# Second attention: one head of each pair normalised by GpSimd, the last piece of the transposed weights copied by VectorE, a new order on VectorE; the convolution in five PSUM banks

## The reference, cut to what matters

```python
for each of 16 heads, for the "selected" and the "window" branch:
    logit = q @ k.T + bias                       # 512 x 512, causal
    p     = softmax(logit)
    o    += gate[head, branch] * (p @ v)
# third branch: 31 compressed keys per query, softmax, gate, @ v_cmp
o = concat(heads) @ w_o
```

## Time and profile before

| | us |
|---|---|
| median of 3 runs | 1904.03 (1902.29 to 1905.01) |
| the profiled execution | 1903.93 |
| its span | 1902.1 |
| TensorE busy | 1876.1 |
| VectorE busy | 985.3 |
| ScalarE busy | 759.2 |
| GpSimd busy | 755.7 |

### The profile page before, as it was taken

How to read it: one execution, slowest core, us unless ns; L and a number is a source line. 1 busy time by engine, 2 the same in 40 slices (tenths; PEclk the granted TensorE clock), 3 DMA queues, 4 the chain that set the end, 5 groups by cost and what they waited for, 6 DMA issues and landing times.

```text
span 1902.1 us, 25390 instructions
## 1 busy us (share of the span) xinstructions
PE 1876.1 (99%) x9404; PEld 1536.4 (81%) x9404; DVE 985.3 (52%) x1647; ACT 759.2 (40%) x1306; POOL 755.7 (40%) x321
## 2 busy tenths in 40 slices
PE   9999999999999999999999999999999999999998
PEld 8887788888888888888888888898766688888886
DVE  7766379354345643335433434754798443443444
ACT  7777454222233532233222222433599632222221
POOL 2321434544444345444544443455300144454452
PEclk9999999999999999999999999999999999999999
DMA  5111313323232134963333232234011123223231
GB/s 205 56 56 34 96 53 112 111 90 101 96 99 91 65 104 93 197 165 100 100 104 99 95 99 89 78 121 147 21 34 57 45 78 111 89 90 107 90 98 57
DMA packets 52526, 177.55 MB, mean 93 GB/s; under 512 B 5559, under 2 KB 5943, under 8 KB 52440
## 3 DMA queue, kind: packets, MB, share of 16 engines
q1 hardware_dynamic: 48240, 166.22, 26.7%
q10 hardware_dynamic: 4200, 10.15, 3.6%
HBM read 166.88 MB, written 9.47 MB: 93 GB/s over the span
## 4 chain that ended last, share of the span: by engine, by line
PE 83%; issue 7%; DVE 5%; ACT 2%; POOL 2%; DMA 0%; DVEq 0%; POOLq 0%
PE ps L445 25%; PE ps L447 25%; PE ps L446 25%; PE ps L963 2%; POOL WL L405 2%; PE ps L904 1%; PE ps L986 1%; DVE arena L2349 1%; DVE arena L2324 1%; ACT arena L1183 1%; PE ps L580 1%; DVE arena L1729 1%; ACT arena L1139 1%; PE ps L877 0%; PE ps L977 0%
## 5 line engine op out<-in xcount | busy, mean ns | idle before, releaser
L405 POOL TENSOR_TENSOR WL<-raw,WH 128x1024 fp32r<-128x1024 f32 x291 | 726.7, 2512 | 1071.6 <-ACT WH L1048 1071.5
L1048 ACT ACTIVATE WH<-raw 128x1024 fp32r<-128x1024 f32 x293 | 302.2, 1054 | 496.2 <-PE ps L447 452.3
L445 PE MATMUL ps<-XH,WH 128*128 128x512 f32 (+1 forms) x1280 | 493.3, 385 | 1.9 <-POOL WL L405 0.8
L447 PE MATMUL ps<-XH,WL 128*128 128x512 f32 (+1 forms) x1280 | 491.1, 384 | 0.0
L446 PE MATMUL ps<-XL,WH 128*128 128x512 f32 (+1 forms) x1280 | 491.1, 384 | 0.0
L445 PE MATMUL ps<-HH,WH 128*128 128x512 f32 x1080 | 423.3, 392 | 0.8 <-DVE HL L2061 0.8
L447 PE MATMUL ps<-HH,WL 128*128 128x512 f32 x1080 | 420.5, 389 | 0.0
L446 PE MATMUL ps<-HL,WH 128*128 128x512 f32 x1080 | 420.3, 389 | 0.0
L445 PEld LDWEIGHTS ps<-XH,WH 128*128 128x128 f32 x1280 | 240.8, 188 | 52.1 <-POOL WL L405 2.9
L447 PEld LDWEIGHTS ps<-XH,WL 128*128 128x128 f32 x1280 | 240.7, 188 | 47.9
L446 PEld LDWEIGHTS ps<-XL,WH 128*128 128x128 f32 x1280 | 240.9, 188 | 46.7
(11 more groups left out here) (268 smaller groups left out, 1719.3 us busy)
## 6 DMA issues: line engine op xcount, KB each, us to landing
raw<-in_weights SPq DMA_DIRECT2D x299, 512.0 KB, 3.5
tab<-arena ACTq DMA_DIRECT2D x1, 5120.0 KB, 76.5
arena<-tab SPq DMA_DIRECT2D x16, 256.0 KB, 2.9
ftab<-arena ACTq DMA_DIRECT2D x1, 2080.0 KB, 23.4
h<-in_xT SPq DMA_DIRECT2D x8, 256.0 KB, 6.4
out_T<-h SPq DMA_DIRECT2D x8, 256.0 KB, 2.2
raw<-in_weights SPq DMA_DIRECT2D x4, 256.0 KB, 4.8
arena<-ftab ACTq DMA_DIRECT2D x4, 256.0 KB
```

What stands on the lines that cost most here:

```text
L405: nc.gpsimd.tensor_tensor(WL[:, s, :], raw[:, s, :], WH[:, s, :].bitcast(f32), SUB)\
L445: nc.tensor.matmul(out, wh, xh, start=start, stop=False)
L447: return nc.tensor.matmul(out, wl, xh, start=False, stop=stop)
L1048: nc.scalar.activation(WH[:, s, :], raw[:, s, :], ACT.Copy).then_inc(*m["whi"].tick())
```

## The change

- **Second attention, GpSimd:** the four multiplications that normalise the second head (r = 1) of each job go from VectorE to GpSimd, which waits for the reciprocals and counts in a new semaphore, n2_pool. The reciprocals of both heads stay on VectorE.
- **Second attention, third copy:** the 256-wide copy of each head goes from ScalarE to VectorE (pair_copy_last), with its own semaphore pt_last.
- **Second attention, order on VectorE:** turn n is now: reciprocal and normalisation of n-1's first head, reciprocal of the second, all three logit steps of n, the two third copies of n-1, then c_weights or the split. In the first job the last logit step moves in between the second and the third c_sub.
- **First attention:** the normalisation of n-1's first head moves in front of logits step 0 of n.
- **Convolution:** five banks (4, 5, 6, 0, 1) instead of three; a wait for the last users of banks 0 and 1 is put ahead of the second query projection.
- **Embedding gate:** two identity products instead of eight.
- **First feed-forward:** the two weight units are rounded before the root.

```diff
         KN, KRR = (5, 6, 0, 1), 7
+        CBANK = (4, 5, 6, 0, 1)
@@ gpsimd, after the keys' six subtractions @@
+            for n in range(NP):
+                pool.wait_ge(sems["i2_done"], 2 * n + 2)
+                for qs in range(TT):
+                    a = PAIRS[n].p(n, 1)[:, POFF[qs]:POFF[qs] + P * (qs + 1)]
+                    c = INV + 8 * (n % 2) + 4 + qs
+                    gate = 3 * PAIRS[n].heads[1] + 1 + PAIRS[n].br
+                    nc.gpsimd.tensor_scalar(a, a, small[:, c:c + 1], GT[:, qs, gate:gate + 1], MUL, MUL)\
+                      .then_inc(sems["n2_pool"], 1)
             lower_units(UO["o2"] + 3, NU)
@@ conv_group @@
-                if g >= 3:
-                    pe.wait_ge(sems["ce_done"], PH * (g - 2))
+                if g >= len(CBANK):
+                    pe.wait_ge(sems["ce_done"], PH * (g - len(CBANK) + 1))
+                elif CBANK[g] < 4:
+                    pe.wait_ge(*m["tile_free"].upto())
@@ tensor @@
             ln_columns(acc).then_inc(sems["ln_sum"], 1)
+            pe.wait_ge(sems["ce_done"], PH * (GPE - 1))
             project(1, 3, 2, HH, HL, hooks={3: ln_mean})
...
-            keep_busy(8, (b.t + 3) % 4)
+            keep_busy(2, (b.t + 3) % 4)
@@ late_transposes @@
-                pe.wait_ge(sems["pt_rest"], 4 * (t + 1))
+                pe.wait_ge(sems["pt_last"], 2 * (t + 1))
@@ pair_transposes @@
-                pe.wait_ge(sems["n2_done"], 4 * (j + 1))
+                pe.wait_ge(sems["n2_pool" if r else "n2_done"], 4 * (n + 1))
...
-                        pe.wait_ge(*((sems["pt_g0"], j) if g == 0 else (sems["pt_rest"], 2 * (j - 1) + g)))
+                        pe.wait_ge(sems[("pt_g0", "pt_rest", "pt_last")[g]], j)
@@ scalar @@
+            upper(b.u + 6)
             root(D)
-            upper(b.u + 6)
...
-                for g, (at, w) in enumerate(((0, S), (S, S), (2 * S, 256))):
+                for g, (at, w) in enumerate(((0, S), (S, S))):
@@ vector, first attention @@
             for n in range(NP1 + 1):
+                if n:
+                    mla_normalise(n - 1, 0)
                 if n < NP1:
                     mla_logits(n, 0)
-                if n:
-                    mla_normalise(n - 1, 0)
-                if n < NP1:
                     mla_logits(n, 1)
@@ vector, second attention @@
             for t in range(TT):
+                if t == 2:
+                    pair_logits(0, 2)
                 c_sub(t, 1)
...
+            def pair_copy_last(n, r):
+
+                dve.wait_ge(sems["t2_done"], 3 * (2 * n + r) + 3)
+                V.tensor_copy(PT2[r][:, 2 * S:2 * S + 256], ps[:, TBANK[2], 0:256]).then_inc(sems["pt_last"], 1)
+
             for n in range(NP + 1):
...
+                if n:
+                    pair_inverse(n - 1, 0)
+                    pair_normalise(n - 1, 0)
+                    pair_inverse(n - 1, 1)
...
                     pair_logits(n, 0)
+                    pair_logits(n, 1)
+                    pair_logits(n, 2)
                 if n:
-                    pair_inverse(n - 1, 0)
-                    pair_normalise(n - 1, 0)
-                if 0 < n < NP:
-                    pair_logits(n, 1)
-                if n:
-                    pair_inverse(n - 1, 1)
-                    pair_normalise(n - 1, 1)
-                if n < NP:
-                    pair_logits(n, 2)
+                    for r in range(2):
+                        pair_copy_last(n - 1, r)
                 if 1 <= n < 1 + TT:
                     c_weights(n - 1, 1)
```

More of the change, by code:

```diff
@@ L57 @@
 cmp_done kc_hi kc_lo vc_ok gate_t gate_s gate_ok c_lg c_mx c_bias c_sub c_exp c_sum c_inv c_mul c_tr c_pt krep_hi krep_lo key_lo
-ple_s out_ok out_st s2_done l2_done e2_done i2_done n2_done t2_done pt_g0 pt_rest pv_done pv_out""".split()
+ple_s out_ok out_st s2_done pt_last l2_done e2_done i2_done n2_done n2_pool t2_done pt_g0 pt_rest pv_done pv_out""".split()
 class Mark:
@@ L579, in conv_group @@
                     at = 32 * PH * (LAGS - 1 - k)
-                    last = nc.tensor.matmul(ps[:, 4 + g % 3, 0:P], tz[:, (g + 1) % 4, at:at + P],
+                    last = nc.tensor.matmul(ps[:, CBANK[g % 5], 0:P], tz[:, (g + 1) % 4, at:at + P],
                                             U[:, g, LAGS - 1 - k:UW - k], start=k == 0, stop=k == LAGS - 1)
@@ L979, in pair_values @@
                 for g, kts in enumerate(VALUES):
[L980 to L983, removed]
+                    pe.wait_ge(sems[("pt_g0", "pt_rest", "pt_last")[g]], 2 * n + 2)
                     for kt, at in kts:
@@ L1182, in conv_out @@
                     rows = slice(32 * f, 32 * f + 32)
-                    nc.scalar.activation(cacc[32 * q:32 * q + 32, c, PH - 1 - f::PH], ps[rows, 4 + g % 3, 0:P], ACT.Identity,
+                    nc.scalar.activation(cacc[32 * q:32 * q + 32, c, PH - 1 - f::PH], ps[rows, CBANK[g % 5], 0:P], ACT.Identity,
                                          bias=small[rows, BIAS2 + 4 * q + c:BIAS2 + 4 * q + c + 1]).then_inc(sems["ce_done"], 1)
@@ L2343, in pair_normalise @@
             def pair_normalise(n, r):
-                dve.wait_ge(sems["i2_done"], 2 * n + r + 1)
+                dve.wait_ge(sems["i2_done"], 2 * n + 1)
                 for qs in range(TT):
```

## The result

The changed kernel takes 1908.10 us in the median of 8 executions (1907.05 to 1910.12), the kernel before 1903.91 (1902.29 to 1905.01): a ratio of 1.0024, with a 95% interval of 1.0015 to 1.0033. It is slower by 4.2 us. The prediction was 1911.3, with a range of 1904.5 to 1917.5.

A forecast was written before the change was run, and what follows sets the result against it. TensorE was taken as the bound, busy 1876.1 of 1902.1 us. Terms 0.3 + 4.7 + 3.1 - 0.8 gave +7.3 on 1903.93, 1911.2, and a median of 1911.3 us; range 1904.5 to 1917.5.

The forecast's parts named there:

- The bound and the mechanism: Second attention: TensorE's wait for VectorE's second normalisation goes, a wait for ScalarE's copy replaces it, and exponentials are delayed.
- the circle: Second attention: dependent steps from one start of the second head's transposes to the next, summed to 7.78 us a turn.
- Turns 6 to 15: Second attention, five pairs of turns: 16.18 us a pair against 16.12 now, +0.3 us, bounds -1.5 and +1.8.
- Turns 2 to 5: Second attention: c_weights and ScalarE's compressed-branch copy add 1.25 and 0.33, giving 9.36 us a turn; +4.7 us.
- The start: Second attention, turn 1: last score step waits for logits behind the first normalisation; +3.1 us, bounds +1.5 and +4.7.
- GpSimd: Second attention: its four multiplications take 2.6 us, with 3.7 us available, so they cost nothing in the forecast.
- The gate: Embedding gate: fewer idle products let TensorE start earlier, -0.8 us; bounds -1.7, and +0.8 if the clock comes back later.
- Root and rounding: First feed-forward: the wait behind it hangs on the norm, not the weights; 0 us, bounds -0.2 and +0.1.
- Convolution and first attention: Convolution's bank wait of 1.00 us goes but is waited for later; first attention's new order is hidden; 0 us each.
- The total: Whole kernel: the terms add +7.3 us, giving a median of 1911.3 us, with an 8-in-10 range of 1904.5 to 1917.5.
- the forecast's own range: Whole kernel: 1908 to 1914.5 us, the span given to the forecast itself, with chance 0.62.
- The rival with half of the circle under cover: Second attention: c_weights and first normalisation stay hidden, start and turns 2 to 5 lose 1 to 4 us; 1905-1908; chance 0.12.

The follow-up runs named there:

- e1: The changed kernel with the third copy of each head back on ScalarE: 1904.12 us, ratio 0.9997 to the kernel before.
- e4: The changed kernel with the second head's four multiplications back on VectorE, behind those of the first: 1932.47 us, ratio 1.0150 to the kernel before.
- e3: The changed kernel with c_weights between the second and third logits steps instead of behind the third copies: 1904.85 us, ratio 1.0006 to the kernel before.
- e2: The changed kernel with the first logits of job 1 ahead of the first normalisation, in the first turn alone: 1903.59 us, ratio 1.0002 to the kernel before.
- e6: The kernel before, with only the two weight units rounded ahead of the root at the first feed-forward: 1902.58 us, ratio 0.9994.
- e8: The kernel before, with only GpSimd's four multiplications for the second head moved there; order and third copy as before: 1925.75 us, ratio 1.0107.
- e10: The kernel before, with GpSimd's four second-head multiplications and the second reciprocal ahead of the first normalisation: 1902.50 us, ratio 0.9997.
- e5: The kernel before, with only two identity products instead of eight ahead of the embedding gate: 1904.12 us, ratio 1.0001.
- b1: The changed kernel with job 1's first logits ahead of the first normalisation, third copy on ScalarE and eight gate products: 1900.47 us, ratio 0.9979 to the kernel before.

## Why the prediction was right, and where it was not

**The bound and the mechanism** held. The wait for VectorE's second normalisation went, and a wait for ScalarE's copy took its place; the exponentials start when the normalisation ahead of the logits is done. e1 (the circle cut), e4 (more put into it) and e3 (less) show it from three sides.

**Turns 6 to 15: +0.3 forecast, -2.5 measured, outside the bounds of -1.5 to +1.8.** This step failed by two terms of the circle. From the start of the transposes to VectorE's copy I summed 1.31 + 0.32 = 1.63 us. It is 1421.19 to 1422.51, 1.32: the 0.32 was read behind a 384-wide product, and behind the last 128-wide transpose it is 0.11 from TensorE's next instruction, which itself starts 1.21 after the transposes, not 1.31. The second reciprocal delays the logits by 0.08 us (1424.49 to 1424.57), not 0.2. All other terms were within 0.08. Together 7.38 instead of 7.78, so that in the even turns, with the split's 0.62, the circle (8.0 by this sum) is shorter than TensorE's own 8.26 and doesn't show. A sum that lay 0.06 us beside the old rhythm could turn its sign on such terms; the bounds of 0.15 us a turn were too narrow for terms taken from unlike instructions.

**Turns 2 to 5: +4.7 forecast, +2.8 measured**, inside the bounds. The same 0.4 us a turn is missing. What was said of c_weights and of the copy for the compressed branch stands: 7.38 + 1.25 + 0.33 = 8.96, measured 8.87, and e3 took 3.25 us of it away.

**The start: +3.1 forecast, +4.3 measured**, inside the bounds. The step itself started 3.4 us late (1371.32 for 1368.53, and the kernel had been 0.6 us ahead). The other 0.9 lies between it and turn 2, 7.32 us where it had been 6.45, and is the clock: at 1.2 GHz from 1369.6 to 1376.5, before from 1368.5 to 1371.9. In the four other profiles with this order and GpSimd's part the start added 3.1 to 4.2 us. e2 shows that the order was the cause.

**GpSimd** needed 2.39 us; I took 2.6. Its instructions are 772 ns for 512 columns and 452 for 128, so 0.83 ns a column and 0.35 us for each instruction. By the Trainium skill, "GPSIMD Engine Reference", § 4.1 Engine selection, an operation with one input runs at about line rate; at the page's 1.2 GHz that is, as an estimate, 0.83 ns a column, and the trace agrees.

**The gate: -0.8 forecast, +0.6 measured**, at the edge of the bounds, which had named this case. The step that failed is that I took the clock's low stretch for fixed: the wait saved was about right (0.5 to 0.8), and the lower clock lasted 10.2 us instead of 6.8.

**Root and rounding: 0 forecast, -1.1 measured, outside the bounds of -0.2 to +0.1.** I looked at the one wait beside the edit, at 283.57, and not at what ScalarE's list does behind it: the next low part, 12 us later, was late by 0.83 us. e6 shows it alone.

**Convolution and first attention: 0 forecast, 0.0 measured for both.** The changed kernel has TensorE 0.57 us earlier at 94 us, and waits 1.06 us at 102.62 where it had waited 0.51 at 102.82: what is won at the bank is waited for at the lag products, which VectorE ends at 102.52. The 0.2 us that the table has up to here stand already at 10 us, ahead of both parts. No run changes either part alone; this is read from the two traces.

**The total** was right in sign and within the range. The errors of the terms were -2.8, -1.9, -1.1, +1.4 and +1.2 us; that they cancelled in part is luck, and 1908.1 lies just at the lower end of the forecast's own range, 1908 to 1914.5. The rival with half of the circle under cover gave nearly the time, 1905 to 1908, but not for its reason: nothing was covered; the steady turns got shorter.

## What to carry to other kernels

When work is moved between engines, look for the circle that a new wait closes: an instruction that must wait for a late product (here a copy) holds back everything behind it on its engine, and small work put behind it (c_weights, 1.25 us) costs in full, while the same work where the engine waits anyway is free. Sum such a circle from rows of the same kind of instruction, since eight terms that are off by 0.05 us each decide when its length is near the old rhythm. And when an engine's order changes, follow its list to the next use that could be late, not only to the next wait.

## What the runs showed of the hardware

**The clock can fall in a loop that is busy.** In e8 TensorE was busy 10.75 of 13 us and its longest waits were 2.1 us, and the granted clock fell to half three times, which cost 9 to 10 of the 22 us. The sum of waits alone had given 9. That such waits are the reason is an inference: in e10, without them, it didn't fall, and behind the fourth of them in e8 it didn't either.

**It can fall without a gap ahead, too.** Busy times by stretch in the changed kernel at the start of the second attention (same columns):

```profile
1359.40:1362.80 3.40, 3.40 (x31) 3.07 (x32) 2.52 (x14) 3.40 (x13) 3.40 (x3) 1.00 0.00 0
1362.80:1366.20 3.40, 3.27 (x22) 2.71 (x24) 3.06 (x9) 1.26 (x4) 2.56 (x3) 0.50 0.00 0
```

TensorE is busy all of the first stretch, mostly with 64-column products, and the clock is at half in the second. In the kernel before it did not fall there, with the same products. At this place it fell in five of the fourteen profiles (changed, e1, e2, e5, b1), and in none of them had TensorE a gap in the 6.8 us ahead. e1's profile has another low stretch, 6.8 us from 166.8 us on, in the first attention, whose code it shares with the changed kernel; there TensorE was busy 2.62 of the 3.4 us ahead, and in the changed kernel, where the clock stayed full, 2.63. All behind it lies 2.4 us later. So one profile may be 1 to 2.4 us off for this reason alone.

**The scatter of the times goes with the granted clock.** In e1's ten executions the clock was 0.995 of full in the mean in the fastest (1901.96 us) and 0.990 in the three slowest (1905.88 to 1905.96), with the others in order between them. The other kernels show the same, less strictly: in e6 0.996 for 1901.04 and 0.992 for 1908.51 us. Two versions that differ by 1 or 2 us are therefore better compared stage by stage, in traces, than by a few times.

**VectorE and GpSimd slow each other where both work in SBUF.** In the changed kernel VectorE's two multiplications by scalars at 283.90 take 1.00 us with GpSimd idle, and the next two take 4.03 with GpSimd at work from 291.78 on:

```profile
283.90 1.00 DVE L1997 TENSOR_SCALAR arena<-arena,vec 128x512 f32<-128x512 f32 x2
...
295.35 4.03 DVE L1997 TENSOR_SCALAR arena<-arena,vec 128x512 f32<-128x512 f32 x2
```

The Trainium skill, "SBUF — State Buffer", § SBUF: two separate sides, describes a pair of ports that VectorE and GpSimd lock for a whole instruction; the trace agrees: each of the two VectorE instructions ends 0.29 us behind one of GpSimd's subtractions (296.85 behind 296.56, 299.38 behind 299.09). An operation with two tensor inputs is slowed as well: L2001 behind them takes 3.54 us for two, where it had taken 1.41 at 284.82. In the second attention of the changed kernel it did not matter: GpSimd's multiplications run beside logits that read PSUM, which kept their lengths. In e10 they run beside VectorE's normalisation, and there GpSimd was the one that lost, 0.66 us.
